# Negated attention scores with row minima, a skewed bias table, and another order of the even mixer's steps

## The reference, cut to what matters

```
la = q_lat . c_sel + rel_bias[t5_bucket(q_pos - sel)]     # only keys that an index score selects (top k)
pa = softmax(where(valid, la, -inf))
lb = q_b . k_b + cum_f[query] - cum_f[key]                # causal
pb = softmax(where(causal, lb, -inf))
```

## Time and profile before

| what | value |
|---|---|
| median of the runs | 1899.77 us |
| the profiled execution's own time | 1900.92 us |
| its span | 1898.9 us |
| TensorE busy | 1858.5 us, 98% |
| VectorE / ScalarE / GpSimd busy | 927.8 / 726.2 / 386.0 us |
| mean granted TensorE clock | 0.991 of full speed |

### The profile page before, as it was taken

How to read it: one execution, slowest core, us unless ns; L and a number is a source line. 1 busy time by engine, 2 the same in 40 slices (tenths; PEclk the granted TensorE clock), 3 DMA queues, 4 the chain that set the end, 5 groups by cost and what they waited for, 6 DMA issues and landing times.

```text
span 1898.9 us, 23351 instructions
## 1 busy us (share of the span) xinstructions
PE 1858.5 (98%) x9766; PEld 1541.0 (81%) x9766; DVE 927.8 (49%) x1501; ACT 726.2 (38%) x1223; POOL 386.0 (20%) x224
## 2 busy tenths in 40 slices
PE   7999988999999999999999999999989999999998
PEld 7788977888888888777888888888768898888886
DVE  5675544232232244885455555522543356555334
ACT  5664434232221243566624434411323144343211
POOL 1533433111110033211141111100244321111000
PEclk9999989999999999999999999999989999999999
DMA  5111032223222232110122232332222322322321
GB/s 200 67 56 68 7 112 89 89 89 107 93 99 101 81 135 94 67 46 23 46 89 89 89 106 94 111 101 98 89 89 89 111 89 90 109 89 98 113 100 67
DMA packets 28764, 170.01 MB, mean 90 GB/s; under 512 B 3386, under 2 KB 5602, under 8 KB 10866
## 3 DMA queue, kind: packets, MB, share of 16 engines
q1 hardware_dynamic: 28660, 168.53, 25.7%
HBM read 166.37 MB, written 2.11 MB: 89 GB/s over the span
## 4 chain that ended last, share of the span: by engine, by line
PE 92%; DVE 4%; ACT 2%; POOL 1%; issue 0%; DMA 0%; SPq 0%; ACTq 0%; DVEq 0%
PE ps L572 27%; PE ps L574 27%; PE ps L573 27%; PE ps L1115 2%; PE ps L1082 1%; PE ps L1078 1%; PE ps L1100 1%; POOL wL L2499 1%; PE ps L652 1%; ACT wH L1286 1%; PE ps L702 1%; PE ps L1041 1%; PE ps L856 0%; PE ps L865 0%; DVE hL L1824 0%; PE ps L846 0%
## 5 line engine op out<-in xcount | busy, mean ns | idle before, releaser
L572 PE MATMUL ps<-hH,wH 128*128 128x512 f32 (+1 forms) x1568 | 603.5, 385 | 5.5 <-POOL wL L2499 1.9
L574 PE MATMUL ps<-hH,wL 128*128 128x512 f32 (+1 forms) x1568 | 591.6, 377 | 0.0
L573 PE MATMUL ps<-hL,wH 128*128 128x512 f32 (+1 forms) x1568 | 591.5, 377 | 0.0
L1817 DVE TENSOR_TENSOR wL<-raw,wH 128x1024 fp32r<-128x1024 f32 (+1 forms) x196 | 240.4, 1266 | 331.6 <-ACT wH L1286 331.6
L1286 ACT ACTIVATE wH<-raw 128x1024 fp32r<-128x1024 f32 (+2 forms) x298 | 290.3, 1023 | 282.6 <-PE ps L574 282.6
L2499 POOL TENSOR_TENSOR wL<-raw,wH 128x1024 fp32r<-128x1024 f32 (+2 forms) x102 | 246.3, 2437 | 655.9 <-ACT wH L1286 655.9
L572 PEld LDWEIGHTS ps<-hH,wH 128*128 128x128 f32 x1568 | 296.3, 189 | 65.7 <-issue 5.9
L574 PEld LDWEIGHTS ps<-hH,wL 128*128 128x128 f32 x1568 | 296.1, 189 | 54.8
L573 PEld LDWEIGHTS ps<-hL,wH 128*128 128x128 f32 x1568 | 296.5, 189 | 51.9 <-issue 1.0
L572 PE MATMUL ps<-wH,aH 128*128 128x512 f32 x528 | 209.0, 396 | 0.0
L573 PE MATMUL ps<-wL,aH 128*128 128x512 f32 x528 | 208.8, 395 | 0.0
(11 more groups left out here) (370 smaller groups left out, 1900.3 us busy)
## 6 DMA issues: line engine op xcount, KB each, us to landing
raw<-in_wbig SPq DMA_DIRECT2D x139, 1024.0 KB, 4.9
rows<-in_rows SPq DMA_DIRECT2D x12, 512.0 KB, 5.9
x<-in_x SPq DMA_DIRECT2D x8, 512.0 KB, 5.6
raw<-in_wbig SPq DMA_DIRECT2D x8, 512.0 KB, 3.5
out<-x SPq DMA_DIRECT2D x4, 512.0 KB, 2.6
near<-u_scratch SPq DMA_DIRECT2D x1, 1024.0 KB, 7.7
raw<-in_wbig SPq DMA_DIRECT2D x1, 1000.0 KB, 7.8
raw<-in_wbig SPq DMA_DIRECT2D x1, 600.0 KB, 10.4
```

The costliest lines, as they stand in the source:

```text
L572: e.matmul(o, hi, m_hi, start=first, stop=False)
L573: e.matmul(o, hi, m_lo, start=False, stop=False)
L574: return e.matmul(o, lo, m_hi, start=False, stop=end)
L1817: e.tensor_tensor(wL[r][:, cs], raw[r][:, cs], wH[r][:, cs].bitcast(F32), ALU.subtract).then_inc(*low_dve.one(c, h))
```

## The change

Both kinds of scores are computed with the opposite sign (scales of -0.125, the index mask and the gates' sum swapped in sign), the mask and bias terms likewise, and VectorE takes row minima of the negated scores. The minimum is then what ScalarE's exp needs as its bias, with scale -1, and the one-column instruction goes. The scratch table is written 128 times, row r at r*385, and read with pitch 384, so that partition p gets the entries from 127 - p on and the reversal on TensorE goes. The 8 I steps in which it stood stay, empty on TensorE. The order string is another one, with the same 156 F, 96 I and 192 A.

```diff
 def even_order():
-    return ("FFFFIFFFFFFFFFFFFFIFFFFFFFFFFFFFFFIFFFFFFFFFFFFFFFFFIFFIFIIFIIFFIIFFIFFIIFFIIFIIIIFFFFIFFFFFFFFIAIIAFFFAIFFFIAFIIIAFIAFA"
-            "AIFFIIAFIAAIAAAFAIFIAFIAIAAAFFFIAIAFAIFIFAFAAFIFAAFFAAFAAIIAIFAAAIFFAFAIAAFAAFIAIAIIFFAAFAAIFIAIIFFIAAAAAAFAFIIAAAIAAAAI"
-            "FFIFFFAFIAFAFFIAIAFAIFAAIFAAFAAIFAAAAAIFAFFFIIAAIAAIFIFFIIFAAFIAAFAFFAAAAIFFIAAAAIAAIAIAIFAAAFAAAFAAAIAIAAAAIFIAAAFAAAAA"
-            "AAAAIAAIAAAAAAAAFAAAAAFAAAAIIAAAAFAAFAAAAAAIAAIAAAAFAAAIAAAAAIAAAAFAAAAAAAAAAFAAFA")
+    return ("FFFFFIFFFFFFFFFFFFIFFFFFFFFFFFFFFFFFFFFFFFFFFFFIFFFFFIFIFFFFIIFFIFFFFIIFFIIFFFFFFIIIFFFFIFFIFIFFIFIIFAAFFIFFFIFAAIIAIAFF"
+            "IFFFAAAIIAAAIIAAAIAAIAIIAIAAFFAAAAIIAAIAAAFIFIIFIFIFFFFFAAIAIFFFFFFIFIFFFFFAAAIAIAIAAAAIAAIAFFFAAAIIAAAIIAAAIIAAIAFFFFFF"
+            "AIAAIAAAAAAFFIAAAIIFFFFAIAAAAIAIAAIIAFIFFFFAAAIFIFFFFFAAAIAAIAIIAAAIAIAAAAIAAIAAAIAAIFFAIAAIIAAAAAAAAAFFFIAAAFAAAAAAIAAA"
+            "FFAAAIAIAAAAAAAAIFAAAIFAAAAAAAAAFAAAFAAAAAAAAAIAIAAAIAIAAAAAAAAAAAFAAAAAAAAAAFAFAAFA")
...
-    u_dram = nc.dram_tensor("u_scratch", (8, 384), F32, kind="Internal").ap()
+    u_dram = nc.dram_tensor("u_scratch", (8, 128 * 385), F32, kind="Internal").ap()
...
-                    clear(7)
-                    w.wait_ge(*D["near"].at())
-                    w.wait_ge(*D["anti"].at())
-                    e.matmul(ps[7][:, 0:256], anti[:, :], near[:, h, :], start=True, stop=True).then_inc(*lat.pe.one("near", h))
-                    bank[7] = [lat.dve.at("bias", h, 3)]
...
-            e.activation(uu[:, :], ps[7][0:8, 0:384], ACT.Copy).then_inc(*res.act.one("table"))
+            e.activation(uu[:, :], ps[7][0:8, 0:384], ACT.Copy, scale=-1.0).then_inc(*res.act.one("table"))
...
-                        w.wait_ge(*unit.dve.at("neg", u))
-                        e.activation(quarter[s][:, 0:wd], quarter[s][:, 0:wd], ACT.Exp, bias=sx2[:, s, 0:1], accum_out=sx2[:, s, 1:2]).then_inc(*unit.act.one("exp", u))
+                        w.wait_ge(*unit.dve.at("min", u))
+                        e.activation(quarter[s][:, 0:wd], quarter[s][:, 0:wd], ACT.Exp, bias=sx2[:, s, 0:1], scale=-1.0, accum_out=sx2[:, s, 1:2]).then_inc(*unit.act.one("exp", u))
...
-                                               ALU.mult, ALU.add).then_inc(*idx.dve.one("acc", i, h))
+                                               ALU.mult, ALU.add if h else ALU.subtract).then_inc(*idx.dve.one("acc", i, h))
...
-                    w.wait_ge(*lat.pe.at("near", h))
+                    w.wait_ge(*D["near"].at())
...
-                        e.scalar_tensor_tensor(mb[h % 2][:, a:a + n], ps[7][:, 256 - n:256], far[:, h:h + 1], k, ALU.subtract, ALU.add).then_inc(*lat.dve.one("bias", h, i))
+                        e.scalar_tensor_tensor(mb[h % 2][:, a:a + n], near[:, h, 256 - n:256], far[:, h:h + 1], k, ALU.add, ALU.add).then_inc(*lat.dve.one("bias", h, i))
...
-                        e.tensor_tensor_reduce(quarter[s][:, 0:wd], ps[2 + u % 2][:, 0:wd], k, 1.0, 2 * NEG, ALU.add, ALU.max, mx).then_inc(*unit.dve.one("max", u))
-                        w.wait_ge(*unit.dve.at("max", u))
-                        e.tensor_scalar(mx, mx, -1.0, None, ALU.mult).then_inc(*unit.dve.one("neg", u))
+                        e.tensor_tensor_reduce(quarter[s][:, 0:wd], ps[2 + u % 2][:, 0:wd], k, 1.0, -2 * NEG, ALU.add, ALU.min, mx).then_inc(*unit.dve.one("min", u))
...
-            e.dma_start(u_dram, uu[:, :]).then_inc(*D["u_out"].one())
+            e.dma_start(bass.AP(u_dram.tensor, 0, [[128 * 385, 8], [385, 128], [1, 384]]), uu[:, :].unsqueeze(1).broadcast_to([8, 128, 384])).then_inc(*D["u_out"].one())
...
-            e.dma_start(anti[:, :], ins["anti"]).then_inc(*D["anti"].one())
...
-            e.dma_start(near[:, :, :], bass.AP(u_dram.tensor, 0, [[1, 128], [384, 8], [1, 256]])).then_inc(*D["near"].one())
+            e.dma_start(near[:, :, :], bass.AP(u_dram.tensor, 127, [[384, 128], [128 * 385, 8], [1, 256]])).then_inc(*D["near"].one())
```

More of the change, by code:

```diff
@@ L249, in even_order @@
 def even_order():
-    return ("FFFFIFFFFFFFFFFFFFIFFFFFFFFFFFFFFFIFFFFFFFFFFFFFFFFFIFFIFIIFIIFFIIFFIFFIIFFIIFIIIIFFFFIFFFFFFFFIAIIAFFFAIFFFIAFIIIAFIAFA"
-            "AIFFIIAFIAAIAAAFAIFIAFIAIAAAFFFIAIAFAIFIFAFAAFIFAAFFAAFAAIIAIFAAAIFFAFAIAAFAAFIAIAIIFFAAFAAIFIAIIFFIAAAAAAFAFIIAAAIAAAAI"
-            "FFIFFFAFIAFAFFIAIAFAIFAAIFAAFAAIFAAAAAIFAFFFIIAAIAAIFIFFIIFAAFIAAFAFFAAAAIFFIAAAAIAAIAIAIFAAAFAAAFAAAIAIAAAAIFIAAAFAAAAA"
-            "AAAAIAAIAAAAAAAAFAAAAAFAAAAIIAAAAFAAFAAAAAAIAAAIAAAAFAAAIAAAAAIAAAAFAAAAAAAAAAAFAAFA")
+    return ("FFFFFIFFFFFFFFFFFFIFFFFFFFFFFFFFFFFFFFFFFFFFFFFIFFFFFIFIFFFFIIFFIFFFFIIFFIIFFFFFFIIIFFFFIFFIFIFFIFIIFAAFFIFFFIFAAIIAIAFF"
+            "IFFFAAAIIAAAIIAAAIAAIAIIAIAAFFAAAAIIAAIAAAFIFIIFIFIFFFFFAAIAIFFFFFFIFIFFFFFAAAIAIAIAAAAIAAIAFFFAAAIIAAAIIAAAIIAAIAFFFFFF"
+            "AIAAIAAAAAAFFIAAAIIFFFFAIAAAAIAIAAIIAFIFFFFAAAIFIFFFFFAAAIAAIAIIAAAIAIAAAAIAAIAAAIAAIFFAIAAIIAAAAAAAAAFFFIAAAFAAAAAAIAAA"
+            "FFAAAIAIAAAAAAAAIFAAAIFAAAAAAAAAFAAAFAAAAAAAAAIAIAAAIAIAAAAAAAAAAAFAAAAAAAAAAFAFAAFA")
 def odd_order():
@@ L433, in build @@
         wuv = R("wuv", [128, 8, 64])
-        anti = R("anti", [128, 128])
         C0 = R.at
@@ L542, in build @@
             "x0", "x1", "x2", "x3", "cols", "pm", "ident", "U", "brow", "lev", "abias", "ssd_nw", "gain", "oneh", "rb", "u_out",
-            "row", "x_again", "ones_q", "ones_k", "CM", "wuk", "wuv", "anti", "far", "near", "cum_q", "cum_k", "sgg", "sgw", "sgb", "out")}
+            "row", "x_again", "ones_q", "ones_k", "CM", "wuk", "wuv", "far", "near", "cum_q", "cum_k", "sgg", "sgw", "sgb", "out")}
         pre, ev, gate, att, ssd, gdn0, gdn1, sums, mix, res, ffn, even, idx, unit, lat, odd, sgu, ln = stages = [
@@ L1092, in units @@
                         score(u % 32 // 4, u % 4, ps[b][:, 0:128 * (u % 4 + 1)]).then_inc(*unit.pe.one("score", u))
-                        bank[b] = [unit.dve.at("max", u)]
+                        bank[b] = [unit.dve.at("min", u)]
                         yield
@@ L1614, in on_tile @@
                         if t == 0:
-                            e.activation(QB[0:64, h, :], ps[t][0:64, :], ACT.Copy, scale=0.125).then_inc(*even.act.one("QB", h))
+                            e.activation(QB[0:64, h, :], ps[t][0:64, :], ACT.Copy, scale=-0.125).then_inc(*even.act.one("QB", h))
                         else:
@@ L1660, in index @@
                     w.wait_ge(*(idx.pe.at("s", 3, 7) if h < 2 else unit.pe.at("score", 32 + 4 * (h - 2) + 3)))
-                    e.activation(ql[h % 2][:, :], ps[PAIR[h % 2]][:, :], ACT.Copy, scale=0.125).then_inc(*lat.act.one("ql", h))
+                    e.activation(ql[h % 2][:, :], ps[PAIR[h % 2]][:, :], ACT.Copy, scale=-0.125).then_inc(*lat.act.one("ql", h))
                     yield
@@ L2244, in on_tile @@
                     w.wait_ge(*prod.at(c, t))
-                    e.tensor_scalar((KB if t else QB)[0:64, h, :], ps[t][64:128, :], 1.0 if t else 0.125, None, ALU.mult).then_inc(*even.dve.one("KB" if t else "QB", h))
+                    e.tensor_scalar((KB if t else QB)[0:64, h, :], ps[t][64:128, :], 1.0 if t else -0.125, None, ALU.mult).then_inc(*even.dve.one("KB" if t else "QB", h))
                 return on_tile
@@ L2289, in index @@
                     w.wait_ge(*idx.dve.now())
-                    e.tensor_scalar(selm[:, sel_at[i]:sel_at[i] + n], sco[:, 0:n], TAKEN / 2, NEG, ALU.is_gt, ALU.mult).then_inc(*idx.dve.one("sel", i))
+                    e.tensor_scalar(selm[:, sel_at[i]:sel_at[i] + n], sco[:, 0:n], TAKEN / 2, -NEG, ALU.is_gt, ALU.mult).then_inc(*idx.dve.one("sel", i))
                 yield
@@ L2302, in index @@
                         if h > 1:
-                            w.wait_ge(*unit.dve.at("max", 32 + 4 * (h - 2) + i))
-                        e.scalar_tensor_tensor(mb[h % 2][:, a:a + n], ps[7][:, 256 - n:256], far[:, h:h + 1], k, ALU.subtract, ALU.add).then_inc(*lat.dve.one("bias", h, i))
+                            w.wait_ge(*unit.dve.at("min", 32 + 4 * (h - 2) + i))
+                        e.scalar_tensor_tensor(mb[h % 2][:, a:a + n], near[:, h, 256 - n:256], far[:, h:h + 1], k, ALU.add, ALU.add).then_inc(*lat.dve.one("bias", h, i))
                     yield
@@ L2798, in index @@
                 w.wait_ge(*idx.dve.at("negcum"))
-                e.dma_start(QB[65:66, :, :], f1).then_inc(*D["cum_q"].one())
-                e.dma_start(KB[64:65, :, :], f0).then_inc(*D["cum_k"].one())
+                e.dma_start(QB[65:66, :, :], f0).then_inc(*D["cum_q"].one())
+                e.dma_start(KB[64:65, :, :], f1).then_inc(*D["cum_k"].one())
                 yield
@@ L2875, in shape_constants @@
     i, j = np.arange(128)[:, None], np.arange(128)[None, :]
-    out = {"ident": np.eye(128, dtype=f), "anti": np.eye(128, dtype=f)[::-1], "triu": (i <= j).astype(f)}
+    out = {"ident": np.eye(128, dtype=f), "triu": (i <= j).astype(f)}
     r, c = np.arange(128)[:, None], np.arange(256)[None, :]
@@ L2890, in shape_constants @@
```

(2 more changed lines are left out.)

## The result

| | before | after |
|---|---|---|
| median of the runs, us (16 each, taken together) | 1900.07 (1899.09 to 1901.74) | 1904.65 (1901.95 to 1905.1) |
| profiled execution, time / span, us | 1900.92 / 1898.9 | 1904.65 / 1902.9 |
| scratch write issued, us into the span | 291.10 | 290.30 |
| first feed-forward tile on ScalarE | 337.81 | 344.66 |
| the even walk's first and last matmul border | 709.23, 935.61 | 716.10, 939.54 |

The change makes the kernel 0.21% slower: ratio 1.0021, 95% interval 1.0013 to 1.0028. I had forecast 1896.6 us, with a range up to 1900.4. The checkpoints tell where the time went. From the scratch write's issue to the first feed-forward tile it takes 54.36 us for 46.71 before: +7.65. The walk is 2.94 us shorter. The write is issued 0.8 us sooner (scatter of the first stage), and the two stretches between and behind these add 0.09. Together +4.0 us of span.

The account below looks back on a forecast made before the run. TensorE was taken as the bound. Reversal -3.6, sign instruction -0.2, order +0.3 and +0.3 us sum to -3.2, from 1899.77 to 1896.6 us; range 1894.7 to 1900.4 us.

Parts of the forecast that it names:

- The scratch write: Write before the feed-forward, grown from 12 to 1536 KB: 12 to 15 us, hidden under 46 us of cover, cost 0.
- my signs: Checks in the changed profile: write landed before 330 us; forecast wrong if the time between 291 and 341 us changes.
- My rival on the write: Scratch write on one engine: 123 us less 46 of cover, 1977 us in all; chance 0.04.
- The reversal: Eight 128x256 matmuls go from TensorE in the even walk, nothing taking their place: gain 3.6 us, bounds 3.4 to 4.1.
- The sign instruction: 64 one-column VectorE instructions go, one of them on the chain near the walk's end: gain 0.2 us, bounds 0 to 0.76.
- the minimum: VectorE's row minimum in place of the maximum: no difference, bounds -0.15 to +0.15 us each, beside TensorE.
- The bias from SBUF: VectorE's bias instructions read SBUF instead of PSUM: 0 to +0.06 us each in quiet, 0 on the path.
- The order: Longer runs without F in the even walk: TensorE loses 0.3 us after the 91st F and 0.3 after the 152nd.
- the rival that made the kernel slower that way: VectorE falls over two units behind TensorE in runs without F: 1905.9 us, or 1903 with slack; chance 0.10.
- Reading `near`: The table's read keeps 1024 rows of 1 KB and has from 696 to 866 us to land: cost 0.

Follow-up runs that it names:

- e8: The changed kernel with the 1536 KB scratch write made twice, one behind the other, into two scratch tables: 1933.49 us, 1.018 of before.
- e11: The changed kernel with 112 and then 96 copies of the table written in place of 128: 1899.87 and 1896.20 us.
- e7: The changed kernel with 12 KB written to HBM first, then the table HBM to HBM, 128 copies outermost, at the same place in the queue: 1897.19 us.
- e4: The kernel before with the large write, the read at pitch 384 and no reversal; old signs and order: 1904.12 us, 1.0023 of before.
- e10: The kernel before with the large-write table, no reversal and the new order, but old signs, maxima and sign instruction: 1904.26 us, 1.0022 of before.
- e5: The kernel before with only the new order string: 1907.75 us, 1.0041 of before, walk 233.52 us.
- e3: The changed kernel with only the old order string put back: 1904.68 us, 1.0024 of before, walk 223.54 us.
- e2: The changed kernel with the same 1536 KB write issued after chunk 18's load and before chunk 19's: 1896.44 us, 0.9981 of before.

## Why the prediction was wrong, step by step

**The scratch write: the step that failed.** I took 12 to 15 us against a cover of 46 us, and priced it at 0. Both terms were wrong, and one of them put right alone would not have saved the step: 31 us against a cover of 46, and 15 us against 25.8, both come out as hidden.

*Its length* was 31 us (30.3 by e8). My ends, 11.6 and 123 us, held it. I took the lower one from the read of `near`, which the nearest row in bytes is, but not in shape: that transfer has 128 partitions on one side, this one eight on both. The middle that I worked out myself, 15 us over eight engines, rested on packets of the small write that the stretches of the earlier trace rows show only in part. The Trainium skill's figures ("SBUF — State Buffer", section "Door 1: The DMA port swizzle": two ports of 27.2 GB/s for partitions 0 to 7) had given an estimate of 29 us. The trace agrees, 49 to 54 GB/s. I had written that estimate down, and it changed nothing, because of the cover.

*The cover* was the real mistake. I measured it to the first instruction that waits for the table, 337.81, and to the cast of "the next chunk but one", 340.75. But the next load in the queue is issued 5.8 us behind the write, and its chunk is cast at 316.91, a row that I had not read into the argument. From the write's issue to that cast are 25.8 us (316.91 - 291.10). With 31 us of write, 31 + 0.7 of start + 3.7 for the second half (322 to 325.7) is 35.4 us, less 25.8: 9.6 us of wait, and 9.55 are measured. Of these 1.9 cost nothing in sum, which only the result tells: by e11's rows 2.8 us are in hand, 0.4 come back on VectorE, and the clock took up to 0.65. With my 12 to 15 us the write would have been hidden, as e7 shows; with the 29 us of the estimate, 2 us less than the 31, an estimate of 5.7 us would have been lost, 1902.3 us in all. So the estimate was enough to forecast a slower kernel, had I put it against the right row. Of my signs one held and said nothing: the write was over by about 322 us, before my 330. The other, the time between 291 and 341 us, changed. "It would still be hidden" was the false sentence.

My rival on the write was sized by one engine, 1977 us. The mechanism, a write too long for its cover, was the one that came; its price, 7.65 us for the rival's 77, was a tenth.

**The reversal: right in kind, smaller.** 3.6 us of matmuls went, but e4 gives 2.65. Some 0.4 us came back as ScalarE's wait at head 4, and the rest I could not assign row by row. "Nothing takes their place" was too strong: where TensorE gets faster, the next engine on the chain comes up.

**The sign instruction, the minimum: right.** Forecast 0.2, measured 0.17 (e10 against after). The forecast of no difference for the minimum stands with it; they were not run apart, but the row of the minimum has 550 ns for the maximum's 554 in the earlier trace rows:

```profile
L2320 DVE CUSTOM_DVE_ANT_0 rows<-ps,CM 128x384 f32<-128x384 f32 x8 | 4.4, 550 | 1.6 <-PE ps L1072 1.6
```

**The bias from SBUF: right.** Its group after, with mean ns 484 for the 476 of the earlier trace rows:

```profile
L2298 DVE SCALAR_TENSOR_TENSOR mb<-near,far,selm 128x256 f32<-128x256 f32 x24 | 10.3, 484 | 0.0
```

+0.008 us each lies in the 0 to 0.06 that I gave. Beside GpSimd's copies head 0's took up to 0.61; my bound there was 1.2 us for them together. What I missed is a gain: it gives up bank 7, without which the new order would have cost 7 us (e5).

**The order: no loss, where I had forecast 0.6 us.** Measured: 0.1 us better than the old one (e3, e4 against e10). TensorE's waits in the walk of after are 1.3 us, for 0.3 before and 0.7 in e3:

```profile
PE ps L1040 <- ACT rel L1647: 0.6, 1, 0.6
PE ps L1076 <- ACT ql L1655: 0.4, 1, 0.4
PE ps L1094 <- ACT Pt L1681: 0.3, 1, 0.3
```

So the order adds 0.6 us of waits to e3's, as forecast, and the walk is no longer for it; what it gains elsewhere no row of these waits shows. The first wait is in the run after the 91st F: I had taken 0.3 of bounds 0 to 2.9. It goes back, by way of ScalarE's copy, to an index sum. VectorE's index sum stood beside GpSimd's low half, as said, in the timelines of VectorE and GpSimd:

```profile
793.16 2.52 DVE L2274 SCALAR_TENSOR_TENSOR sco<-rel,widx,CM 128x384 f32<-128x384 f32 x1
```

```profile
790.54 4.73 POOL L2491 TENSOR_TENSOR wL<-raw,wH 128x1024 fp32r<-128x1024 f32 x2 [8.69 <-ACT wH L1280]
```

No other wait of the walk was traced to VectorE's load, and the rival that made the kernel slower that way was wrong: in the stretches of the earlier trace rows TensorE lacks 0.59 and 0.31 us of what it had.

```profile
776.00:840.00 64.00, 63.41 (x328) 47.07 (x326) 54.09 (x164) 38.21 (x99) 14.23 (x6) 1.00 0.15 50
...
900.00:936.00 36.00, 35.26 (x226) 27.58 (x225) 17.98 (x81) 28.53 (x88) 0.00 (x0) 1.00 0.00 1
```

**Reading `near`: right.** It landed in 8.7 us for 7.7, with no one waiting.

In sum the walk gave 2.94 us where I had forecast 3.2. That is in part luck: the reversal gave about 1 us less than forecast, and the order 0.7 more. The version with the write behind the load (e2), 1896.44 us, is what I had forecast for the change, and beats both kernels.

## What to carry to other kernels

When a transfer grows, its cover is not the time until its own data is wanted, but until the data of the first load queued behind it is wanted; read that consumer's row. If several estimates of a length disagree by a factor of two, put each against the nearest deadline before you call it hidden. The write from eight partitions was long for its size: 31 us for 1536 KB. Placed behind the urgent load it cost nothing (e2), and neither did it from HBM to HBM with 128 rows outermost (e7).

## What the runs showed of the hardware

A write of 1536 KB from eight partitions ran at 49 to 54 GB/s and a DMA share of 0.44 (31 us); from HBM to HBM with 128 outermost it took 12.1 us, 130 GB/s. The later load on the same queue went ahead on the engines that the write left free (132 GB/s beside 51), and stood in line on the others (29.67 us to landing). VectorE's `xn` with two large inputs in SBUF took 3.42 and 2.30 us beside GpSimd's low half, and 1.28 without it. In e5 TensorE waited 3.5 us for instructions that read PSUM bank 7 before it was free again; behind the longest wait, 2.11 us, the clock was granted at half for some 3.4 us.
